# Pair scan, steps 0 to 3: one projection piece placed ahead of the BT U product instead of behind it

## Time and profile before

| what | value |
|---|---|
| median of 3 runs | 2332.75 us (2332.74 to 2333.16) |
| the profiled execution's own time | 2334.61 us |
| its span, first to last instruction | 2332.8 us |
| PE busy | 2274.4 us, 97% |
| DVE busy | 1224.7 us, 52% |
| ACT busy | 1153.2 us, 49% |
| POOL busy | 1357.0 us, 58% |
| mean granted clock of PE | 0.994 |

### The profile page before, as it was taken

The page is one execution under the profiler, slowest core; times in us unless marked ns, Lnnn a source line. Parts: engine busy times, 40 slices in busy tenths (PEclk is TensorE's granted clock), DMA queues, the critical chain, the costliest instruction groups (busy, mean ns, idle before and its releaser), DMA issues.

```text
span 2332.8 us, 60081 instructions
## 1 busy us (share of the span) xinstructions
PE 2274.4 (97%) x23364; PEld 1940.0 (83%) x23364; DVE 1224.7 (52%) x2450; ACT 1153.2 (49%) x1977; POOL 1357.0 (58%) x566
## 2 busy tenths in 40 slices
PE   6999999999999999999999999999999999999998
PEld 4687787778877888899999888888888888888887
DVE  2388778887883332465565455454434533333322
ACT  3244544454454433444444555555555555555554
POOL 1113223322332534488888877878778877778786
PEclk8999999999999999999999999999999999999999
DMA  9922112111211222267766545545545545455453
GB/s 390 378 95 68 40 66 70 65 50 51 69 65 59 98 84 99 100 244 249 265 238 244 183 168 179 171 169 174 172 171 178 183 163 177 172 178 173 171 180 135
DMA packets 101391, 360.75 MB, mean 155 GB/s; under 512 B 11200, under 2 KB 14784, under 8 KB 101216
## 3 DMA queue, kind: packets, MB, share of 16 engines
q1 hardware_dynamic: 100016, 356.89, 43.5%
q10 hardware_dynamic: 1200, 1.25, 0.2%
HBM read 356.00 MB, written 2.10 MB: 154 GB/s over the span
## 4 chain that ended last, share of the span: by engine, by line
PE 89%; DVE 2%; ACT 1%; issue 0%; DVEq 0%; ACTq 0%
PE ps L223 33%; PE ps L224 17%; PE ps L678 5%; PE ps L196 4%; PE ps L680 4%; PE ps L679 4%; PE ps L198 4%; PE ps L197 4%; PE ps L808 1%; PE ps L793 1%; PE ps L829 1%; PE ps L979 1%; PE ps L843 1%; PE ps L964 1%; PE ps L786 1%; PE ps L1001 1%
## 5 line engine op out<-in xcount | busy, mean ns | idle before, releaser
L187 POOL TENSOR_TENSOR wlo<-raw,whi 128x1024 fp32r<-128x1024 f32 x555 | 1351.6, 2447 | 924.6 <-ACT whi L178 891.7
L223 PE MATMUL ps<-acts,whi 128*128 128x512 f32 x3072 | 1090.6, 399 | 0.0
L224 PE MATMUL ps<-acts,wlo 128*128 128x256 f32 x3072 | 858.0, 279 | 0.0
L178 ACT ACTIVATE whi<-raw 128x1024 fp32r<-128x1024 f32 x562 | 591.9, 1054 | 278.3 <-PE ps L224 140.7
L223 PEld LDWEIGHTS ps<-acts,whi 128*128 128x128 f32 x3072 | 576.4, 188 | 132.1 <-DVE acts L2806 0.3
L224 PEld LDWEIGHTS ps<-acts,wlo 128*128 128x128 f32 x3072 | 579.5, 189 | 0.9
L678 PE MATMUL ps<-acts,whi 128*128 128x512 f32 (+1 forms) x560 | 211.7, 378 | 1.2 <-DVE W L1561 0.8
L680 PE MATMUL ps<-acts,wlo 128*128 128x512 f32 (+1 forms) x560 | 189.9, 339 | 0.0
L679 PE MATMUL ps<-acts,whi 128*128 128x512 f32 (+1 forms) x560 | 189.8, 339 | 0.0
L196 PE MATMUL ps<-acts,whi 128*128 128x256 f32 (+1 forms) x576 | 181.7, 315 | 0.0
L198 PE MATMUL ps<-acts,wlo 128*128 128x256 f32 (+1 forms) x576 | 180.0, 313 | 0.0
(11 more groups left out here) (390 smaller groups left out, 3043.8 us busy)
## 6 DMA issues: line engine op xcount, KB each, us to landing
raw<-stream SPq DMA_DIRECT2D x564, 512.0 KB, 3.2
W<-stream SPq DMA_DIRECT2D x64, 512.0 KB, 9.0
graw<-stream SPq DMA_DIRECT2D x32, 512.0 KB, 4.6
W<-xT SPq DMA_DIRECT2D x4, 1024.0 KB, 8.8
XR<-xT SPq DMA_DIRECT2D x16, 128.0 KB, 5.5
outT<-XR SPq DMA_DIRECT2D x3, 512.0 KB, 3.6
cns<-consts SPq DMA_DIRECT2D x1, 928.0 KB, 9.4
cns<-consts SPq DMA_DIRECT2D x1, 896.0 KB, 7.5
```

The lines of the kernel that those rows point to most:

```text
L178: nc.scalar.activation(high, raw[slot], ACT.Copy).then_inc(hi_done, 1)
L187: nc.gpsimd.tensor_tensor(wlo[slot], raw[slot], whi[slot].bitcast(F32), ALU.subtract).then_inc(lo_done, 1)
L223: nc.tensor.matmul(both_parts, whi[slot][:, k, :], hl[:, :, k0 + k, :], start=first and k == 0, stop=False)
L224: ins = nc.tensor.matmul(ps[:, bank, 0:T], wlo[slot][:, k, :], hl[:, 0, k0 + k, :], start=False, stop=last and k == UK - 1)
```

```diff
-        FILL = ((2, 0, 2),) * 7 + ((2, 2, 0),)
+        FILL = ((2, 1, 1),) * 4 + ((2, 0, 2),) * 3 + ((2, 2, 0),)
         FILL_LAST = ((1, 0, 1),) * 8
```

## The result

The changed kernel takes 2341.42 us (median of 8 runs, 2338.47 to 2343.95); the kernel before, run beside it, 2332.95. That is 8.5 us slower by the medians. The forecast was 2341.5.

The account below looks back on a forecast made before the run. PE, busy for 97% of the span, was taken to bound the kernel. Delays of DVE behind POOL left each of seven scans 1.25 us longer, 8.75 us on the 2332.75 us median: 2341.5 us, range 2330 to 2344.5.

Parts of the forecast that it names:

- The sum: Seven scans at 1.25 us each, 8.75 us more in all, on the 2332.75 us median: 2341.5 us.
- PE alone: Term and rival: only PE's filled waits and switches count; 0.65 us a scan gained, 2328.2 us; chance 0.12.
- State 1: Pair 1: one more DVE tap falls behind POOL, so L964 of step 2 starts at 272.72 us against 272.56.
- State 3: Before step 4: more DVE work falls behind POOL, state 3 starts 0.8 us later; 0.13 us of gain left.
- State 5: Before step 6: L1398 and L1403 are each held behind a POOL instruction; L964 of step 6 starts 1.25 us later.
- The margin: On DVE before step 6: L1398 was to start 0.14 to 0.22 us behind POOL's instruction and be held.
- the lost race: Rival: POOL loses one of two races, L1398 or L1403 goes first; 0.9 us gained in all, 2331.8 us; chance 0.30.
- The list of what would show it: Signs in the new profile: L1001's 21 waits gone, L964 waits about 0.1, 0.4, over 1 us, L1398 about 3.4 us.

Follow-up runs that it names:

- step1_only: Kernel before with only step 1 of FILL set to (2, 1, 1); 2337.53 us, ratio 1.0019.
- dve_eased_no1: Changed kernel with state 5 ahead of L1403 and three taps moved on DVE, step 1 back at (2, 0, 2); 2328.47 us, ratio 0.9976.
- dve_eased: Changed kernel with state 5 ahead of L1403, two taps moved ahead of state 0 and one behind state 3; 2329.52 us, ratio 0.9979.
- the DVE moves alone: Kernel before, old FILL table, with state 5 ahead of L1403, two taps ahead of state 0, one behind state 3; 2332.99 us, ratio 0.9999.
- late_unit7: Changed kernel with a one-column ACT instruction ahead of unit 7's rounding, to delay POOL's request; 2334.34 us against 2334.16 of before, ratio 0.9999.
- state5_first: Changed kernel with DVE's L1403 moved behind state 5 instead of ahead of it; 2335.57 us, ratio 1.0006.
- step2_only: Kernel before with only step 2 of FILL set to (2, 1, 1); 2339.74 us, ratio 1.0026.
- step0_only: Kernel before with only step 0 of FILL set to (2, 1, 1); 2336.74 us, ratio 1.0013.

## Why the prediction was right

*The sum.* Forecast 8.75 us, measured 8.5 by the medians and 9.07 in the seven scans of the profiled execution. Seven scans at 1.25 us were forecast; six cost 1.51 us each, and one cost 0.04. The dearer scans and the one that was lost nearly cancel, so that the sum came within 0.3 us is in part luck.

*PE alone.* A lone piece was costed at 0.18 us of switches. step1_only has 0.19 at step 2, and dve_eased_no1 against dve_eased 0.19. The expected rest, 0.65 us a scan, was 0.74 in dve_eased, where no wait of L964 or L1001 is left in these scans (the DVE moves alone give 0.03). The term was right, and its gain was put a little low.

*State 1.* L964 of step 2 was to be 0.16 us late and is 0.23.

*State 3.* The wait in step 4 was to be 0.4 us and is 0.54; the 0.13 us that I left of the gain is zero: step 4 starts at 18.82 in both kernels. L1314 is the instruction in question there; it started 0.03 us behind POOL and lost, which the forecast had left open.

*State 5.* L964 of step 6 was to be 1.25 us late and is 1.50, with its wait of 1.39 us. L1398 and L1403 are both long, as forecast. Most of what was missing is one delay, from the end of a state to L964, which was taken 0.09 us too short; it counts at step 4, on which POOL's request hangs, and again at step 6.

*The margin was mis-sized.* I put L1398 0.14 to 0.22 us behind POOL; it is 0.06. Two terms make up the difference. L1392's end does overlap the state, as the lower figure allowed: from the end of state 3 (283.52) to L1398 (287.52) it is 4.00 us, against 4.08 in the forecast. And I took 0.06 us from the end of a state to L964. The trace of after shows 0.15: state 3 ends at 283.05 + 0.47 = 283.52 and L964 starts at 283.67; state 5 ends at 294.64 and L964 starts at 294.79. POOL's request hangs on L964, so it too came 0.09 later than I had it. The forecast stood on the right side of a race that was closer than I knew, and in one scan of the seven it went the other way. There L1398 started 0.05 us behind POOL and still won. The timelines of DVE and POOL of that scan:

```profile
365.33 1.21 DVE L1398 SCALAR_TENSOR_TENSOR W<-W 128x1024 f32<-128x1024 f32 x1
```

```profile
365.28 3.52 POOL L187 TENSOR_TENSOR wlo<-raw,whi 128x1024 fp32r<-128x1024 f32 x1 [7.61 <-ACT whi L178]
```

That scan is 38.08 us, 0.04 over before. It is the lost race of the prediction, for which 0.13 us of gain a scan was expected and none was found. It had been given 0.30, and the race was close: with POOL 0.09 us later against DVE it was the result in all seven scans, as late_unit7 shows. The argument against it, that a start 0.03 us behind POOL's is enough to lose, was too strong: in the same trace of the kernel before, L1441 won at 0.03 (its lines stand at the end).

*The list of what would show it* held but for one scan: L1001's 21 waits are gone, L964 waits in steps 2, 4 and 6, and L1398 takes 3.4 us, in six scans where seven were forecast. The waits are longer than listed, 0.19, 0.54 and 1.39 us.

The Trainium skill, "SBUF — State Buffer", section "SBUF: two separate sides", has the rule for the port pair on which this rests, that the first to start holds it for the whole instruction. late_unit7 agrees with it: 0.09 us in the order of two starts decides over 1.4 us. The scan in which L1398 won with a start recorded 0.05 us behind POOL's does not fit it as recorded.

## What to carry to other kernels

Idle time on the bounding engine is often the slack of a chain through other engines. Before filling it, follow what the filler delays: here BT U, the state, and the order in which two engines reach a resource they can't share. Then ask of each step by itself whether it had anything to win; one step of the four won. Steps 0 and 2 lost by the chain behind them until DVE's own order was moved along, and step 1, which had no wait to fill, cost 0.19 us a scan even then. Where a start decides by hundredths of a us who goes first, move the short thing that someone waits for ahead of the long one: in state5_first L1398 still lost the race, and step 6 did not wait.

## What was not expected

The point at which DVE loses to POOL is sharp but not where starts are equal. In the changed kernel L1398 won 0.05 us behind POOL in one scan and lost at 0.06 in pair 1 and at 0.05 in another scan (596.92 against 596.87), in step2_only it won at 0.04 (595.99 against 595.95) and lost at 0.06, while L1314 lost at 0.03 and, in a later stage, so did L2162. L1441, later in a scan, starts 0.03 us behind POOL and goes both ways. In the kernel before, pair 1, it won (the timelines of DVE and POOL):

```profile
299.40 0.41 DVE L1441 TENSOR_TENSOR W<-W 128x256 f32<-128x256 f32 x1
```

```profile
299.37 2.68 POOL L187 TENSOR_TENSOR wlo<-raw,whi 128x1024 fp32r<-128x1024 f32 x1
```

In the changed kernel, first pair, it lost:

```profile
223.81 2.62 DVE L1441 TENSOR_TENSOR W<-W 128x256 f32<-128x256 f32 x1
```

```profile
223.78 2.37 POOL L187 TENSOR_TENSOR wlo<-raw,whi 128x1024 fp32r<-128x1024 f32 x1
```

So a start that is recorded 0.05 us later can still be first, and which of the two records is off, or whether it depends on the instruction that ran before, these runs do not tell. That the spread of the changed kernel's runs, 2338.5 to 2344.0 us, comes from how many scans win this race would fit its price of 1.47 us a scan, but no run shows it; the kernel before spread as widely without such a race.

L964 starts 0.15 us after the end of the DVE instruction that it waits for, while L730 starts 0.05 us after L1372 (274.86 + 0.67 = 275.53, then 275.58, in step0_only). The forecast used 0.06, near the shorter figure, for L964.
